# Gate products in two fp32r halves, with GpSimd making the weighted one-hots

## The reference

```
sc   = q . sub_keys                      # two sets of 128 scores per head
v1,i1 = top_k(sc[0], 16); v2,i2 = top_k(sc[1], 16)
top_v, top_pos = top_k(v1 + v2 pairs, 16)
eidx  = i1 * 128 + i2  (of the picked pairs)
gates = softmax(top_v)
a   = gelu(u_tab[eidx] . x) * gates
out = sum_k a_k * v_tab[eidx_k]
```

## Time and profile before

| quantity | value |
|---|---|
| median of three executions | 2060.76 us |
| profiled execution, its own time | 2065.37 us |
| span of its trace | 2063.4 us |
| busy TensorE, VectorE, ScalarE, GpSimd | 98%, 72%, 51%, 1% |
| mean granted clock of TensorE | 0.987 |

### The profile page before, as it was taken

How to read it: one execution, slowest core, us unless ns; L and a number is a source line. 1 busy time by engine, 2 the same in 40 slices (tenths; PEclk the granted TensorE clock), 3 DMA queues, 4 the chain that set the end, 5 groups by cost and what they waited for, 6 DMA issues and landing times.

```text
span 2063.4 us, 43464 instructions
## 1 busy us (share of the span) xinstructions
PE 2018.4 (98%) x12678; PEld 1805.7 (88%) x12678; DVE 1487.8 (72%) x3743; ACT 1054.8 (51%) x2059; POOL 27.7 (1%) x56
## 2 busy tenths in 40 slices
PE   7989999999999999999999999999999999999997
PEld 6748899999999877777779689999999998888886
DVE  5662778877777688888875348786777767777776
ACT  2032245755555555555544424566555555555554
POOL 0000000000000000000000000000000000000000
PEclk9999999999999999999989999999999999999998
DMA  9861288865655899999820333777565577777774
GB/s 377 343 236 46 87 279 288 251 189 177 175 171 175 277 325 327 322 328 323 279 102 31 154 117 121 229 219 212 172 176 175 171 207 245 242 240 241 241 242 150
DMA packets 170904, 446.79 MB, mean 217 GB/s; under 512 B 19024, under 2 KB 85840, under 8 KB 166880
## 3 DMA queue, kind: packets, MB, share of 16 engines
q1 hardware_dynamic: 163472, 392.65, 59.6%
q0 software_dynamic: 7376, 53.45, 6.6%
HBM read 409.32 MB, written 36.70 MB: 216 GB/s over the span
## 4 chain that ended last, share of the span: by engine, by line
PE 94%; ACT 2%; DVE 2%; DMA 1%; issue 1%; DVEq 0%; ACTq 0%; SPq 0%
PE bank L492 93%; ACT big L931 1%; DMA big<-in_w_mod 1%; PE bank L631 1%; DVE raw L1097 0%; DVE big L1192 0%; PE bank L811 0%; DMA cst<-in_consts 0%; DVE big L1114 0%; DVE wmod_ring L1114 0%; DVE x_lo L1106 0%; DVE big L1527 0%; ACT L991 0%; ACT big L949 0%; ACT raw L878 0%
## 5 line engine op out<-in xcount | busy, mean ns | idle before, releaser
L1356 DVE TENSOR_TENSOR lo<-raw,hi 128x512 fp32r<-128x512 f32 x1024 | 702.5, 690 | 346.4 <-ACT hi L985 342.1
L985 ACT ACTIVATE hi<-raw 128x512 fp32r<-128x512 f32 x1024 | 642.8, 630 | 444.1 <-PE bank L492 430.2
L492 PE MATMUL bank<-x_hi,hi 128*128 128x256 f32 x2152 | 622.2, 289 | 3.9 <-ACT x_hi L876 1.8
L492 PE MATMUL bank<-x_hi,lo 128*128 128x256 f32 x2152 | 610.1, 283 | 0.0
L492 PE MATMUL bank<-x_lo,hi 128*128 128x256 f32 x2152 | 606.1, 283 | 0.0
L492 PEld LDWEIGHTS bank<-x_hi,hi 128*128 128x128 f32 x2152 | 413.6, 192 | 6.8 <-issue 4.2
L492 PEld LDWEIGHTS bank<-x_hi,lo 128*128 128x128 f32 x2152 | 413.6, 192 | 0.0
L492 PEld LDWEIGHTS bank<-x_lo,hi 128*128 128x128 f32 x2152 | 411.7, 192 | 0.0
L492 PE MATMUL bank<-hi,a_hi 128*128 128x512 f32 x1024 | 401.3, 392 | 3.4 <-issue 1.7
L492 PE MATMUL bank<-hi,a_lo 128*128 128x512 f32 x1024 | 398.8, 389 | 0.0
L492 PE MATMUL bank<-lo,a_hi 128*128 128x512 f32 x1024 | 398.4, 389 | 0.0
(11 more groups left out here) (159 smaller groups left out, 1344.4 us busy)
## 6 DMA issues: line engine op xcount, KB each, us to landing
raw<-in_u SPq DMA_DIRECT2D x256, 512.0 KB, 3.9
raw<-in_v SPq DMA_DIRECT2D x256, 512.0 KB, 4.6
s_store<-work SPq DMA_DIRECT2D x256, 128.0 KB, 3.7
wmod_ring<-s_store SPq DMA_DIRECT2D x256, 128.0 KB, 3.7
wmod_ring<-in_w_mod SPq DMA_DIRECT2D x54, 512.0 KB, 5.7
big<-in_w_mod SPq DMA_DIRECT2D x40, 512.0 KB, 6.3
big<-in_w_q POOLq DMA_DIRECT2D x16, 1024.0 KB, 7.1
big<-in_w_in POOLq DMA_DIRECT2D x6, 2048.0 KB, 14.4
```

The source lines that it names most:

```text
L492: return nc.tensor.matmul(o, w, x, start=start, stop=stop, skip_group_check=free)
L985: f(hi[:, r % 2, c], raw[:, r, c], ACT.Copy).then_inc(s[l]["hi_done"], 1)
L1356: v.tensor_tensor(lo[:, r % 2, c], raw[:, r, c], hi[:, r % 2, c].bitcast(F32), ALU.subtract).then_inc(s[l]["lo_done"], 1)
```

## The change

The gate value is cut in an upper fp32r part (`pick[:, 2]`, now rounded on the copy) and a lower rest (`pick[:, 3]`, one new subtraction). For each token there are now two weighted one-hots, upper and lower, side by side in 256 columns of `hot_b`, all tiles of the gate products are fp32r, and one fp32r product of 256 columns per token gives both halves of the table in PSUM. Four tokens need 1024 columns, so the PSUM tensors are now four pairs of two banks; a group takes a whole pair, and groups alternate between two pairs instead of four banks.

VectorE still makes the plain one-hots (`hot_a`). The weighted ones are made by GpSimd, eight instructions of 128 columns per group, in a loop written out over the 64 groups (`weighted`) behind its last transfer of the layer. ScalarE copies the upper half out of PSUM, and VectorE adds the lower half onto it (`sum_gates` for group g - 2, behind `one_hot` of group g). The buffers `hot_a` and `hot_b` are new memory next to and over `a_hi` and `a_lo`; the scratch memory of GpSimd's transfers is set to 8192 bytes to make room for them.

```diff
+        a_parts = sb("a_parts", [P, 12 * T], F32R)
+        a_hi = a_parts[:, 0:2 * T].rearrange("p (a t) -> p a t", t=T)
+        a_lo = a_parts[:, 2 * T:4 * T].rearrange("p (a t) -> p a t", t=T)
+        hot_a = a_parts[:, 0:4 * T].rearrange("p (r t n) -> p r t n", r=2, n=P)
+        hot_b = a_parts[:, 4 * T:12 * T].rearrange("p (r t s n) -> p r t s n", r=2, s=2, n=P)
...
+        pair = [ctx.enter_context(nc.psum_tensor(f"pair{i}", [P, 1024], F32)) for i in range(4)]
+        bank = [pair[i // 2][:, (i % 2) * 512:(i % 2 + 1) * 512] for i in range(8)]
...
@@ gpsimd
+                def weighted(g, wait):
+                    if wait:
+                        pool.wait_ge(s[l]["hot_used"], g - 1)
+                    for n in range(4):
+                        c = slice(4 * g + n, 4 * g + n + 1)
+                        for half in range(2):
+                            ins = nc.gpsimd.tensor_scalar(hot_b[:, g % 2, n, half], iota, pick[:, 1, c], pick[:, 2 + half, c], ALU.is_equal, ALU.mult)
+                    ins.then_inc(s[l]["hotb_ready"], 1)
+
+                pool.wait_ge(s[l]["pick_copied"], 3)
+                for g in range(GROUPS):
+                    weighted(g, g >= 2)
@@ tensor, group
-                        pe.wait_ge(s[l]["g_copied"], g - 3)
+                        pe.wait_ge(s[l]["g_summed"], g - 1)
                     pe.wait_ge(s[l]["hot_ready"], g + 1)
+                    pe.wait_ge(s[l]["hotb_ready"], GROUPS * l + g + 1)
                     for n in range(4):
-                        last = mm(bank[b][:, n * P:(n + 1) * P], hot[b % 2][:, 0, n, :], hot[b % 2][:, 1, n, :])
+                        last = mm(pair[b % 2][:, 2 * n * P:2 * (n + 1) * P], hot_a[:, b % 2, n, :], hot_b[:, b % 2, n].rearrange("p s n -> p (s n)"))
@@ scalar, copy_gates
-                    f(dst, bank[b][:, :].rearrange("p (t j) -> p j t", t=4), ACT.Copy).then_inc(s[l]["g_copied"], 1)
+                    f(dst, pair[b % 2][:, :].rearrange("p (t s j) -> p s j t", t=4, s=2)[:, 0], ACT.Copy).then_inc(s[l]["g_copied"], 1)
@@ vector, one_hot and sum_gates
-                    for n in range(4):
-                        ins = v.tensor_scalar(hot[r % 2][:, 1, n, :], iota, pick[:, 1, bass.ds(4 * g + n, 1)],
-                                              pick[:, 2, bass.ds(4 * g + n, 1)], ALU.is_equal, ALU.mult)
+                def sum_gates(g, r):
+                    dve.wait_ge(s[l]["g_copied"], g + 1)
+                    dst = gates[:, :, bass.ds(4 * g, 4)]
+                    v.tensor_tensor(dst, pair[r % 2][:, :].rearrange("p (t s j) -> p s j t", t=4, s=2)[:, 1], dst, ALU.add)\
+                        .then_inc(s[l]["g_summed"], 1)
@@ vector, ahead of the groups
-                v.tensor_copy(pick[:, 2, :], bank[7][:, 0:T]).then_inc(s[l]["pick_copied"], 1)
+                v.tensor_copy(pick[:, 2, :].bitcast(F32R), bank[7][:, 0:T]).then_inc(s[l]["pick_copied"], 1)
                 dve.wait_ge(s[l]["pick_copied"], 2)
+                v.tensor_tensor(pick[:, 3, :], bank[7][:, 0:T], pick[:, 2, :], ALU.subtract).then_inc(s[l]["pick_copied"], 1)
@@ vector, the step of the groups
                         one_hot(4 * i + r, r)
+                        sum_gates(4 * i + r - 2, r)
...
-    nc = bacc.Bacc("TRN2", target_bir_lowering=False, num_devices=1)
+    nc = bacc.Bacc("TRN2", target_bir_lowering=False, num_devices=1, dynamic_dma_scratch_size=8192)
```

More of the change, by code:

```diff
@@ L167, in build @@
         lo = sb("lo", [P, SPLITS, D], F32R)
-        a_hi = sb("a_hi", [P, 2, T], F32R)
-        a_lo = sb("a_lo", [P, 2, T], F32R)
+        a_parts = sb("a_parts", [P, 12 * T], F32R)
[3 more added lines that the diff above has]
+        hot_b = a_parts[:, 4 * T:12 * T].rearrange("p (r t s n) -> p r t s n", r=2, s=2, n=P)
         wmod_ring = sb("wmod_ring", [P, MODS, D])
@@ L175, in build @@
         stat = sb("stat", [P, 256])
-        pick = wmod_ring[:, 2, 0:3 * T].rearrange("p (a t) -> p a t", a=3)
+        pick = wmod_ring[:, 2].rearrange("p (a t) -> p a t", a=4)
         first_mods = [wmod_ring[:, n] for n in range(MODS)]
@@ L183, in build @@
         fox_maps = wmod_ring[:].rearrange("p a n -> p (a n)")
-        hot = [x.rearrange("p (a t n) -> p a t n", a=2, n=P) for x in (wmod_ring[:, 0], wmod_ring[:, 1])]
         back = wmod_ring[:, 2].rearrange("p (r t) -> p r t", t=T)
-        bank = [ctx.enter_context(nc.psum_tensor(f"bank{i}", [P, 512], F32)) for i in range(8)]
+        pair = [ctx.enter_context(nc.psum_tensor(f"pair{i}", [P, 1024], F32)) for i in range(4)]
+        bank = [pair[i // 2][:, (i % 2) * 512:(i % 2 + 1) * 512] for i in range(8)]
         ident = cst[:, C_ID:C_ID + P]
@@ L307, in build @@
                  "q_ps", "q_copied", "key_ps", "key_copied", "equal_ready", "sel_ready", "pick_copied",
-                 "hot_ready", "hot_used", "g_copied", "hi_done", "lo_done", "w_used",
+                 "hot_ready", "hot_used", "g_copied", "g_summed", "hi_done", "lo_done", "w_used",
                  "s_gelu", "a_ready", "ah_done", "al_done",
@@ L311, in build @@
         s = [{n: sem(f"{n}_{l}") for n in names} for l in range(LAYERS)]
-        for n in ("xh_done", "xl_done", "gate_max", "gate_exp", "pick_ready", "pick_ps"):
+        for n in ("hotb_ready", "xh_done", "xl_done", "gate_max", "gate_exp", "pick_ready", "pick_ps"):
             s[0][n] = s[1][n] = sem(n)
@@ L790, in experts @@
                     up(GROUP_AT + r, r % 2)
-                    group(r, r, False)
+                    group(r, r, r >= 2)
                 with pe.Fori(1, GROUPS // 4) as i:
@@ L798, in experts @@
                         up(2 * i + r, r)
-                pe.wait_ge(s[l]["g_copied"], GROUPS)
+                pe.wait_ge(s[l]["g_summed"], GROUPS)
                 down(0, 0, first=True)
@@ L1038, in _ @@
                 up_steps(32, GROUP_AT)
-                act.wait_ge(s[l]["pick_copied"], 2)
+                act.wait_ge(s[l]["pick_copied"], 3)
                 with act.Fori(0, GROUPS // 4) as i:
@@ L1360, in one_hot @@
                         dve.wait_ge(s[l]["hot_used"], g - 1)
-                    v.tensor_tensor(hot[r % 2][:, 0], iota.unsqueeze(1).to_broadcast([P, 4, P]),
-                                    pick[:, 0, bass.ds(4 * g, 4)].unsqueeze(2).to_broadcast([P, 4, P]), ALU.is_equal)
-                    for n in range(4):
-                        ins = v.tensor_scalar(hot[r % 2][:, 1, n, :], iota, pick[:, 1, bass.ds(4 * g + n, 1)],
-                                              pick[:, 2, bass.ds(4 * g + n, 1)], ALU.is_equal, ALU.mult)
-                    ins.then_inc(s[l]["hot_ready"], 1)
+                    v.tensor_tensor(hot_a[:, r % 2], iota.unsqueeze(1).to_broadcast([P, 4, P]),
+                                    pick[:, 0, bass.ds(4 * g, 4)].unsqueeze(2).to_broadcast([P, 4, P]), ALU.is_equal)\
+                        .then_inc(s[l]["hot_ready"], 1)
+                def sum_gates(g, r):
[3 more added lines that the diff above has]
+                        .then_inc(s[l]["g_summed"], 1)
                 def weigh(j, b, round_):
@@ L1419, in experts @@
                 v.tensor_copy(pick[:, 0:2, :].rearrange("p a b -> p (a b)"), bank[6][:, :]).then_inc(s[l]["pick_copied"], 1)
-                v.tensor_copy(pick[:, 2, :], bank[7][:, 0:T]).then_inc(s[l]["pick_copied"], 1)
+                v.tensor_copy(pick[:, 2, :].bitcast(F32R), bank[7][:, 0:T]).then_inc(s[l]["pick_copied"], 1)
                 dve.wait_ge(s[l]["pick_copied"], 2)
+                v.tensor_tensor(pick[:, 3, :], bank[7][:, 0:T], pick[:, 2, :], ALU.subtract).then_inc(s[l]["pick_copied"], 1)
+                dve.wait_ge(s[l]["pick_copied"], 3)
                 for g in range(4):
@@ L1425, in experts @@
                     one_hot(g, g, g >= 2)
+                    if g >= 2:
+                        sum_gates(g - 2, g)
                 with dve.Fori(1, GROUPS // 4) as i:
@@ L1430, in experts @@
                         one_hot(4 * i + r, r)
+                        sum_gates(4 * i + r - 2, r)
+                for n in range(2):
+                    sum_gates(GROUPS - 2 + n, n)
                 with dve.Fori((GROUP_AT + GROUPS) // 4, NKEY // 4) as i:
@@ L1434, in experts @@
                             lower(4 * i + r, r, half)
-                dve.wait_ge(s[l]["g_copied"], GROUPS)
+                dve.wait_ge(s[l]["g_summed"], GROUPS)
                 for n in range(2):
```

## The result

The changed kernel takes 2481.9 us against 2062.0 us for the kernel before, each the median of four runs: 1.204 times as long, with a 95% interval of 1.202 to 1.205. The forecast had the sign, and the place of the wait: TensorE waits for GpSimd in front of its gate products. It did not have the size: 88 us more was expected and 420 us came, far above the range of 2004 to 2255 us. The profiled execution has a span of 2475.2 us, 411.8 us more than before.

What follows compares the result with a forecast made beforehand. TensorE, busy 98% of the span, was taken to bound the kernel before; after the change GpSimd would, with 2.06 + 8 x 0.30 = 4.46 us a step against 3.77, over 128 steps +88 us: 2149 us, range 2004 to 2255.

Steps and rivals of the forecast that it cites:

- the sign: Whole kernel: the change makes it slower, given a chance of 0.62.
- TensorE's part: Gate products: 0.89 us a step removed, 0.48 added; a step bound by TensorE takes 3.37 us, 51 us less in all.
- VectorE's part: Weighted one-hots, 1.03 us, removed; addition of 0.75 us, at most 1.5, added; own work 2.8 us a step, at most 3.6.
- ScalarE's part: Copy of the group out of PSUM: same 512 elements and order, 0.60 us; in total 2.2 us a step, no effect.
- GpSimd (a): Length p of one weighted one-hot on GpSimd: 0.30 us, between 0.16 and 0.53; the eight take 2.4 us a step.
- GpSimd (b): SBUF reading beside VectorE: each stands while the other works, so a step costs 2.06 us + 8p.
- rival 1: GpSimd keeps up and TensorE stays the bound: 51 us less, 2010 us; chance 0.32.
- GpSimd (c): GpSimd's other waits: only the rate counts, the start fits into 7 us; smaller scratch memory 0, at most 5 us per layer.
- Rival 4: GpSimd's length and sharing costs both high: 6.3 us a step, +324, 2385 us; chance with its surroundings 0.10.
- Rival 3: GpSimd alone is the bound, without shutting out, from p = 0.47 on; at 0.53 +60, 2121 us; chance 0.07.
- The estimate from GPSIMD Engine Reference: GpSimd's weighted one-hot: 0.11 to 0.22 us for 128 columns, making 2.9 to 3.8 us a step with the sharing rule.

Runs made afterwards that it cites:

- e5_fill: The changed kernel, with GpSimd filling each 128 columns with a constant instead of making weighted one-hots, reading nothing from SBUF: 2019.1 us, one run.
- e7_three: The changed kernel, with weighted one-hots split: VectorE three upper halves, ScalarE their lower halves by a ratio, GpSimd both halves of the fourth token: 2016.2 us, 0.977 times before.
- e1_vector8: The changed kernel, with VectorE making all eight weighted one-hots of a group and GpSimd none: 2153.4 us, 1.044 times before.
- e9_psum: The changed kernel, with VectorE's plain one-hots reading the pick numbers from PSUM instead of SBUF: 2452.5 us, 1.189 times before.
- e6_half: The changed kernel, with GpSimd making only the four lower halves of a group and VectorE the four upper ones: 2103.3 us, 1.020 times before.

## Why the prediction was wrong

- **TensorE's part: right.** 3.37 us a step was forecast; e5_fill and e7_three show 3.36. Of the 51 us to be gained e7_three gets 46.
- **VectorE's part: right.** The addition was taken as 0.75 us; it takes 0.69, and the stride is free. e1_vector8 shows the sum of its instructions to be the step when it is the bound: 2155 us from the sum, 2153 measured.
- **ScalarE's part: right.** Its copy takes 598 ns, 599 before. VectorE's additions wait for it four times, 22 us in all, and none of it is in the chain.
- **GpSimd (a), the length p: wrong, and the step that failed.** Taken as 0.30 us from VectorE's same instruction, bounded by 0.16 and 0.53. It is 0.774 us from start to start when VectorE is not in the way. 8 x (0.774 - 0.30) = 3.8 us a step, or 485 us over 128 steps, was missing. The error was in both bounds' reasoning. An issue of a transfer, taken as the longest thing that GpSimd does, is no bound for a loop over columns. From below, VectorE's slope of 1.04 ns a column was carried to an engine where it is 3.4, and 0.03 us was taken for a fixed part of 0.35.
- **GpSimd (b), the sharing: right in kind, too large in size.** 2.06 us a step was taken, as if no moment of VectorE's reading could be used. The price was 0.81 us. In the changed kernel VectorE is busy for 178 of 446 us and pauses between most of these instructions, so a GpSimd instruction as a rule loses only what is left of one VectorE instruction when it begins to read, and one that reads already is not stopped (497.36). This took 1.25 us a step, 160 us, off again. The two errors together: 4.46 us forecast, 6.98 us from the times (3.77 + 411.8 / 128), 6.91 and 7.01 us measured within the layers. That the sign was right is luck as the forecast reached it. With its p and the real price of sharing the step is 8 x 0.30 + 0.81 = 3.2 us, under TensorE's 3.37, and rival 1 would have been forecast, 2010 us. In the kernel it is the other way round: even with no sharing, 8 x 0.774 = 6.2 us is far over 3.77. A slip without effect on the sum: a weighted one-hot reads `iota` and two scalars, not three.
- **GpSimd (c), other waits: right.** The first group starts at 435.3 instead of 434.5 us. Beyond what its steps explain, 2063.4 - 128 x 0.41 = 2011 us, e7_three's span of 2015.1 us is 4 us longer; that is the most that the smaller scratch memory can be read to cost, and no run takes it alone.
- **The rivals.** Rival 4, a high p together with sharing, was nearest in mechanism and in time, with 2385 us; it had 0.10 and was left out of the range. Rival 3, GpSimd alone as the bound, had 0.07. Its condition, 8p over 3.77 us, holds, but VectorE's lengths are not unchanged (684 to 721 ns). Both were held to need p near its upper bound of 0.53, which itself is too low.

The rule of SBUF — State Buffer (the Trainium skill, § Who interferes with whom) on VectorE instructions with two SBUF inputs held here where it was tried: they and GpSimd's reads hold each other up (e9_psum), a fill is not held up (e5_fill), and the addition with an input in PSUM does no harm (the instruction at 669.44). VectorE's weighted one-hots have one tensor input and are held up too, and hold up GpSimd, by about 0.05 us (e6_half); no run shows whether that comes from their scalars or from how they read `iota`. The estimate from GPSIMD Engine Reference (the Trainium skill, § Performance pitfalls for Q7 kernels, where 2.03 and 1.03 cycles are given for compare and select), 0.11 to 0.22 us for the columns, did not hold: the measured slope of 3.4 ns gives 0.43 us for 128 columns.

## What to carry to other kernels

Where an engine has no compute row in the trace, its rate is the largest unknown of a move to it; one look at such an instruction is worth more than a bound borrowed from another engine, and a forecast without it needs a range up to several times the borrowed value. The gain on the busiest engine was real here, and it was the placing of 8 small instructions that turned -51 into +420 us; spread over three engines by lengths that had been measured, they fit. The price of sharing is neither nothing nor the whole time that the other engine reads. For each GpSimd instruction it was 0.10 us where VectorE was busy 40% of the stage (the changed kernel), 0.24 us at 90% (e6_half) and 0.53 us at 99% (e7_three): a fuller VectorE made it dearer.

## What was not expected of the hardware

- A GpSimd comparison and product over 128 columns of fp32 with two per-partition scalars takes 0.774 us from start to start, VectorE's 0.26 us. With constants it is 0.70 us, with one scalar and one operation 0.58 us. By recorded length 128 columns take at least 0.782 us, 256 columns 1.212 us, and a fill of 128 columns 0.194 us.
- An fp32r product of 128 columns takes 0.11 us on TensorE and one of 256 columns 0.12 us; a full fp32 product of 128 columns, issued as two instructions, takes 0.22 us.
- VectorE's plain one-hots are 721 ns long beside GpSimd's reads and 684 ns with one input in PSUM: the sharing costs both sides. A GpSimd instruction that begins to read ahead of VectorE is not lengthened; one that begins behind it waits, and through several VectorE instructions if they follow without a pause (2.22 us in e7_three).
